# Inputs with the contracted dimension first, and expert values as 512 moving columns, in a one-core decoder-layer step

## What is computed

```python
z = h @ w_in                                  # [a | u | v], token mixing, then @ w_out, layer norm
mk, mv = mem_prompt @ w_mk, mem_prompt @ w_mv # 256 memory rows
s = einsum('bthd,bmhd->bhtm', h @ w_mq, mem_k)        # prompt: mk; samples: cache_mem_k
h = layer_norm(ALPHA * h + softmax(s) @ mem_v @ w_mo)
# expert layer: 8 heads pick 16 of 128*128 experts per token
act = gelu(einsum('thkd,td->thk', peer_u[eidx], xb))
out = einsum('thk,thkd->td', gate * act, peer_v[eidx])
h = layer_norm(ALPHA * h + out)
```

## Time and profile before

| what | value |
|---|---|
| median of 3 runs | 3913.64 us (3912.26 to 3916.97) |
| the profiled execution's own time | 3911.4 us |
| its span, first to last instruction | 3909.7 us |
| mean granted clock of PE | 0.986 of 2.4 GHz |
| PE busy / weight loads | 96% / 94% |
| DVE, ACT, POOL busy | 66%, 34%, 22% |
| chain that ended last, by engine | PE 89%, DVE 4%, DMA 3%, ACT 2% |

### The profile page before, as it was taken

The page is one execution under the profiler, slowest core; times in us unless marked ns, Lnnn a source line. Parts: engine busy times, 40 slices in busy tenths (PEclk is TensorE's granted clock), DMA queues, the critical chain, the costliest instruction groups (busy, mean ns, idle before and its releaser), DMA issues.

```text
span 3909.7 us, 61245 instructions
## 1 busy us (share of the span) xinstructions
PE 3772.0 (96%) x23909; PEld 3664.8 (94%) x23909; DVE 2585.0 (66%) x3393; ACT 1324.3 (34%) x1615; POOL 860.6 (22%) x534
## 2 busy tenths in 40 slices
PE   8998999989889989999999999999899999999997
PEld 6788999989859989999999999999899999999997
DVE  3323334352463366689888477778799989889896
ACT  3343222241442242233555322222233333333334
POOL 0000023300002300066000121223333333433440
PEclk9999999999999999999999999999999999999999
DMA  6541333323543322344455999999999999999994
GB/s 225 204 147 51 89 83 83 92 66 118 215 151 86 86 67 76 100 148 148 146 189 192 356 397 398 398 397 378 385 407 414 400 402 398 370 412 411 400 397 149
DMA packets 392373, 941.45 MB, mean 241 GB/s; under 512 B 24484, under 2 KB 264800, under 8 KB 340120
## 3 DMA queue, kind: packets, MB, share of 16 engines
q1 hardware_dynamic: 340640, 565.78, 41.6%
q0 software_dynamic: 51616, 374.19, 23.6%
HBM read 865.84 MB, written 72.77 MB: 240 GB/s over the span
## 4 chain that ended last, share of the span: by engine, by line
PE 89%; DVE 4%; DMA 3%; ACT 2%; issue 1%; DVEq 1%; POOL 0%; SPq 0%; ACTq 0%
PE pp L200 24%; PE pp L1218 24%; PE pp L1265 13%; PE pt L1265 7%; PE pl L1265 7%; PE pt L1192 2%; PE pp L844 2%; DMA u_raw<-in_peer_ut 1%; PE pt L844 1%; PE pl L844 1%; DVE vs_lo L1868 1%; DVE gbuf L2073 1%; PE pl L1140 1%; PE pp L1069 1%; PE pt L927 1%
## 5 line engine op out<-in xcount | busy, mean ns | idle before, releaser
L1218 PE MATMUL pp<-h_hi,ut_hi 128*128 128x384 f32 x2048 | 704.3, 344 | 4.2 <-DVE ut_lo L1969 4.2
L1218 PE MATMUL pp<-h_lo,ut_hi 128*128 128x384 f32 x2048 | 690.8, 337 | 0.0
L1218 PE MATMUL pp<-h_hi,ut_lo 128*128 128x384 f32 x2048 | 688.9, 336 | 0.0
L229 DVE TENSOR_TENSOR w_lo<-raw,w_hi 128x2048 fp32r<-128x2048 f32 x116 | 266.5, 2298 | 447.3 <-ACT w_hi L210 447.3
L1969 DVE TENSOR_TENSOR ut_lo<-u_raw,ut_hi 128x1024 fp32r<-128x1024 f32 x256 | 331.6, 1298 | 250.2 <-ACT ut_hi L1583 171.3
L1615 ACT ACTIVATE v_hi<-v_raw 128x1024 fp32r<-128x1024 f32 x256 | 271.8, 1062 | 657.6 <-PE pp L1265 477.7
L1218 PEld LDWEIGHTS pp<-h_hi,ut_hi 128*128 128x128 f32 x2048 | 386.0, 188 | 5.6 <-DVE ut_lo L1969 5.2
L1218 PEld LDWEIGHTS pp<-h_lo,ut_hi 128*128 128x128 f32 x2048 | 385.9, 188 | 0.0
L1218 PEld LDWEIGHTS pp<-h_hi,ut_lo 128*128 128x128 f32 x2048 | 385.2, 188 | 0.0
L2096 DVE TENSOR_TENSOR v_lo<-v_raw,v_hi 128x1024 fp32r<-128x1024 f32 x256 | 313.5, 1225 | 103.6 <-ACT v_hi L1615 102.6
L210 ACT ACTIVATE w_hi<-raw 128x2048 fp32r<-128x2048 f32 x116 | 222.0, 1913 | 388.9 <-PE pp L200 260.8
(11 more groups left out here) (431 smaller groups left out, 7879.5 us busy)
## 6 DMA issues: line engine op xcount, KB each, us to landing
u_raw<-in_peer_ut SPq DMA_DIRECT2D x256, 512.0 KB
v_raw<-in_peer_v SPq DMA_DIRECT2D x256, 512.0 KB
p_f<-p_scr SPq DMA_DIRECT2D x64, 768.0 KB
raw<-in_w_in SPq DMA_DIRECT2D x24, 1024.0 KB, 5.7
g_scr<-gs POOLq DMA_DIRECT2D x6, 4096.0 KB, 13.8
raw<-in_w_mk SPq DMA_DIRECT2D x16, 1024.0 KB, 4.8
raw<-in_w_mv SPq DMA_DIRECT2D x16, 1024.0 KB, 4.8
raw<-in_w_out SPq DMA_DIRECT2D x16, 1024.0 KB, 5.9
```

The source lines that it names most:

```text
L229: nc.vector.tensor_tensor(w_lo[:, s], raw[:, s], w_hi[:, s].bitcast(F32), ALU.subtract).then_inc(lo_ready, 1)
L1218: last = mm(pp[0][:, d, 0:N], w[:, d, k, :], x[:, k, S:S + N], start=(k == 0 and w is ut_hi and x is h_hi), stop=(k == KC - 1 and w is ut_lo))
```

## The change

Host side: x, mem_prompt and cache_mem_k are handed over with the contracted dimension in the partitions. All turns of rows, and of cached keys, are gone; ACT and DVE split from the loaded tile. x is split between the splits of panels 18 to 21. The order of k's turn and the start of the w_in panels stays otherwise.

```diff
-            for n in range(2):
-                rows_load(n)
+            sp.dma_start(quarter(mem_raw, 0), quarter(a["mem_t"], 0)).then_inc(mem_in[0], 16)
             panel_load(streams[0][1], 0)(num(1), 1)
+            for n in range(1, 4):
+                sp.dma_start(quarter(mem_raw, n), quarter(a["mem_t"], n)).then_inc(mem_in[n], 16)
...
-                    for m in range(2, len(row_tiles) - 1):
-                        rows_load(m)
+                    for m in range(4):
+                        sp.dma_start(quarter(x_raw, m), quarter(a["x_t"], m)).then_inc(x_in, 16)
...
+                    for m in range(2 * DB):
+                        if m >= 4:
+                            sp.wait_ge(kr_d, 2 * (m - 3))
+                        sp.dma_start(ckt[:, m % 4]..., a["cache_kt"][m // 2, m % 2]).then_inc(ckt_in[m % 4], 16)
+                        if m == 5:
...
+                if st == 0 and k % NG == 0:
+                    pe.wait_ge(rows_l, k // NG + 1)
...
+            def x_out(n):
+                act.wait_ge(x_in, 64)
+                f(quarter(h_hi, n), quarter(x_raw, n), ACT.Copy).then_inc(rows_h, 1)
...
-                f(kr_hi[n % 3][:, :, :], (pt2, pl)[n % 2]..., ACT.Copy)
+                f(kr_hi[n % 3][:, :, :], ckt[:, n // 2 % 4, n % 2], ACT.Copy).then_inc(kr_a, 1)
```

```diff
+            def value_tile(s, b, d, t):
+                for p, v in ((p_hi, v_hi), (p_hi, v_lo), (p_lo, v_hi)):
+                    for h in range(2):
...
+                        last = mm(acc_bank(s, t, h), p[:, d, t * P:(t + 1) * P], v[:, d, h * 512:(h + 1) * 512],
+                                  start=(b == 0 and p is p_hi and v is v_hi), stop=(b == NK - 1 and p is p_lo))
...
+            def own_rows(s):
+                pe.wait_ge(r_ready, KC + 1)
+                for t in range(ND):
+                    for c in range(8):
+                        mm(acc_bank(s, t, c // 4)[:, c % 4 * P:(c % 4 + 1) * P],
+                           r[:, 8 * s + c, S + t * P:S + (t + 1) * P], ident[:, :], start=False, stop=False)
...
-            pe.wait_ge(acc_done, KC)
             for t in range(ND):
...
+                for d in range(4):
+                    pe.wait_ge(lo_done, 2 * (2 * NK - 4 + d + 1))
+                    value_tile(1, NK - 4 + d, d, t)
...
+            for t in range(ND):
+                for h in range(2):
+                    act.wait_ge(vd_done, 2 * (ND + t) + h + 1)
+                    last = f(row_part(1, t, h), acc_bank(1, t, h)..., ACT.Copy,
+                             accum_out=rst[:, 2 + t, 1 + h:2 + h])
+                last.then_inc(ln_act, 1)
+                row_square(2 + t, row_tile(t))
                 row_std(2 + t, P)
...
-            for c in range(8, KC):
-                add_out(c)
```

More of the change, by code:

```diff
@@ L365, in program, with quarter @@
         mem_lo = at("mem_lo", Y_HI + KC * MEM * 4, [P, KC, MEM], FR)
[L366 to L370, removed]
-        NG = KC // 4
[L373 to L377, removed]
+        mem_raw = at("mem_raw", H_LO, [P, KC, MEM])
+        x_raw = at("x_raw", Y_LO, [P, KC, T])
+        NG = KC // 4
+        def quarter(x, n):
+            return x[:, NG * n:NG * (n + 1), :]
         kv_nat = [at("k_nat", TMP, [P, MT, D]), at("v_nat", Y_HI, [P, MT, D])]
@@ L818, in _ @@
             mm, turn = nc.tensor.matmul, nc.tensor.transpose
[L819 to L833, removed]
             def memory_rows(st, k):
@@ L1072, in _ @@
             pe.wait_ge(evacuated, MO0)
[L1073 to L1077, removed]
+            for n in range(DB * AH):
+                cache_scores(n)
             pe.wait_ge(two_ready, 2)
@@ L1252, in values @@
             def values(s, i, d):
-                m = i * 4 + (s * NK + d)
                 b = i * 4 + d if isinstance(i, int) else None
                 pe.wait_ge(lo_done, i * 8 + 2 * (s * NK + d + 1))
[L1257 to L1268, removed]
+                for t in range(ND):
+                    last = value_tile(s, b, d, t)
@@ L1277, in _ @@
+            for d in range(4):
+                values(0, 0, d)
+            with pe.Fori(1, NK // 4 - 1) as i:
+                for d in range(4):
+                    values(0, i, d)
+            own_rows(0)
+            for d in range(4):
+                values(0, NK // 4 - 1, d)
+            for d in range(4):
+                values(1, 0, d)
+            own_rows(1)
+            with pe.Fori(1, NK // 4 - 1) as i:
                 for d in range(4):
-                    values(s, NK // 4 - 1, d)
@@ L1281, in _ @@
-            pe.wait_ge(acc_done, KC)
+                    values(1, i, d)
             for t in range(ND):
[L1283 to L1288, removed]
+                for d in range(4):
+                    pe.wait_ge(lo_done, 2 * (2 * NK - 4 + d + 1))
+                    value_tile(1, NK - 4 + d, d, t)
@@ L1327, in _ @@
                             .then_inc(evacuated, 1)
-            for n in range(MT, len(row_tiles)):
-                rows_out(n)
             for g in range(8):
@@ L1611, in v_split @@
                     if e == 3:
-                        act.wait_ge(vd_done, 8)
+                        for t in range(ND):
+                            for h in range(2):
+                                act.wait_ge(vd_done, 2 * t + h + 1)
+                                f(row_part(0, t, h), acc_bank(0, t, h).rearrange("p (c n) -> p c n", n=P), ACT.Copy,
+                                  accum_out=rst[:, 2 + t, h:h + 1]).then_inc(acc_done, 1)
                 else:
@@ L2129, in _, with mean_of @@
             base = done[0]
-            def mean_of(t, n, parts):
+            def mean_of(t, n):
                 dve.wait_ge(ln_act, ACT_LN[f"sum{t}"])
                 x = rst[0:n, t]
-                for k in range(1, parts):
-                    tt(x[:, 0:1], x[:, 0:1], x[:, k:k + 1], ALU.add)
+                if t >= 2:
+                    stt(x[:, 0:1], x[:, 0:1], x[:, 1:2], x[:, 2:3], ALU.add, ALU.add)
                     dve.drain()
@@ L2147, in row_gain, with row_bias @@
                 stt(x, x, rst[0:n, t, 3:4], gain, ALU.add, ALU.mult)
-            def row_bias(t, n, x, bias):
+            def row_bias(t, n, x, bias, out=None):
                 dve.drain()
-                stt(x, x, rst[0:n, t, 6:7], bias, ALU.mult, ALU.add).then_inc(row_ready, 1)
-            def row_out(t, n, x, gain, bias):
-                row_gain(t, n, x, gain)
-                row_bias(t, n, x, bias)
+                stt(x if out is None else out, x, rst[0:n, t, 6:7], bias, ALU.mult, ALU.add).then_inc(row_ready, 1)
             def by_chunk(x):
@@ L2189, in _ @@
             for m in range(2, 2 * NK):
-                if m == NK + 3:
-                    for c in range(8):
-                        add_out(c)
+                if m == NK + 5:
+                    dve.wait_ge(acc_done, 2 * ND)
+                    tt(rst[:, 2:5, 0:1], rst[:, 2:5, 0:1], rst[:, 2:5, 1:2], ALU.add)
+                    dve.drain()
                 v_split(m)
```

231 lines of the change are left out of this document (105 added, 126 removed).

## The result

| | before | after |
|---|---|---|
| median of the runs, us | 3912.95 (4 runs, 3909.51 to 3916.97) | 3870.16 (4 runs, 3867.26 to 3872.23) |
| ratio after / before | | 0.9893, 95% interval 0.9881 to 0.9905 |
| profiled execution, us (its span) | 3911.40 (3909.7) | 3867.26 (3865.5) |

The change gains 42.8 us where 66 were forecast; 3870.2 lies just above the range of 3834 to 3870.

A forecast was written before the change was run, and what follows sets the result against it. PE, working 96% of the span, was taken as the bound. Terms 5.5 + 12.9 + 17.4 + 21.6 - 5.4 + 14.2 = 66.2 us took 3911.4 to 3845.2 us profiled, 3847 as a median; range 3834 to 3870.

The forecast's parts named there:

- the part on the values: Value products: 18 matmuls of 512 columns replace 24 of 384 per block; minus 21.6 us, bounds 8 and 28.
- Columns alone set the pace: Rival on the values: 512 columns take 231.5 ns, the block stays at 4.167 us; 3869 us, chance 0.05.
- Own rows: Values: 48 added float32 matmuls of 128 columns at 0.113 us; plus 5.4 us, bounds 3.1 and 10.9.
- start: Kernel start: PE begins 10.2 us sooner, but panel 6 is ready near 55; minus 5.5 us, bounds 0 and 10.2.
- turns of x: Between v's evacuation and the first w_in panel: x split during panels 18 to 21; minus 12.9 us, bounds 10 and 14.
- tail: Behind PE's last product: 13.7 us instead of 29.1, less 1.1 for stalls; minus 14.2 us, bounds 8 and 17.
- cached keys: Cached-key scores: turns gone, DVE and then DMA limit, scores end at 1047.5; minus 17.4 us, bounds 23.3 and 4.
- the stop for a load behind `ktp`: Cached keys: with `ktp` in small pieces before load 6, 3 us of stall are added.
- The rival of the clock: Cached keys run largely at half clock, PE 1.86 us a pair, scores end at 1061; 3860 us, chance 0.10.
- DMA did not cap the values: Rival on the values: DMA caps them and two thirds of the gain would go; 3861 us, chance 0.13.
- Nor did DVE bind there: Rival on the values: DVE becomes the bound, a block at 4.40 us, slower than before; 3925 us, chance 0.02.

The follow-up runs named there:

- e3: The changed kernel with p_lo alone moved by 192 bytes; 3843.60 us in one run, 3850.95 us (ratio 0.9848) when timed again in five runs.
- e5: A separate program, TensorE alone on zero operands at different start offsets, against no kernel; 512 columns took 226.7 ns aligned, up to 233.4 ns otherwise.
- e7: The changed kernel without its products of own rows with the scaled identity; 3862.89 us in one run.
- e8: The changed kernel with the ktp loads issued behind all sixteen loads of cached keys instead of behind the sixth; 3858.45 us in one run.
- e11: The changed kernel with p_lo moved 192 bytes, ktp loads behind all cached keys, and tiles h and y 64 bytes lower; 3837.49 us, ratio 0.9807.
- e2: The changed kernel with the loop over the two 512-column halves moved outside the three value products; 3865.89 us in one run.
- e4: The changed kernel with both the halves loop outside the three value products and p_lo moved by 192 bytes; 3849.83 us in one run.

## Why the prediction was wrong

The step that failed stands in the part on the values: "The extra is 12.0, 13.6 and 13.4 ns, a constant. So a block costs 18 x 226.7 = 4.080 us". The three extras came from three stages with their operands in different places. 13.4 ns was that of the memory rows, whose four tiles start alike; carried to the values it was right for a kernel in which `p_lo` starts alike too (e3: exactly 226.7), and wrong for this one. The values gained 3.4 us instead of 21.6. The rival "Columns alone set the pace" hit the number, 231.5 ns and 3869 us, at a chance of 0.05, and its mechanism was wrong: aligned, 512 columns do take 226.7 (e3, e5). The bounds of the term, 8 and 28 us, were worked out for extras of 16 or 12 ns (16 would leave 9.9, not 8); 17.8 was outside, though the trace of before had a warning: the u products with the same 384 columns stood 175.6 ns apart, the values 173.9. Two paces for one shape say that something besides the shape decides. The prediction took one of them and never set it beside the other.

The Trainium skill ("TensorE: Matmul & The Clock Gate", section "Back-to-back issue gap") gives N/2.4 + 2.5 ns, 215.8 for 512 columns. No order and no place here came under 226.7, so that the trace does not agree. The Trainium skill's page "SBUF — State Buffer", section "Operand start alignment", lets an operand start at any multiple of its element size and says of its runs that they timed nothing; e5 shows that the legal places differ by up to 6.7 ns a matmul.

**Own rows** were mis-sized: 48 products at the price of 48 turns, 5.4 us. A float32 product against the identity takes two records where the turn takes one; 10.7 us by the trace and 9.0 to 10.7 by e7, up to nearly the upper bound of 10.9.

Right, by their own steps: the **start** (5.6 for 5.5, with the spread told above; panel 6 at 55.8 where "near 55" was worked out, the load issued at 40.5 for "near 40"); the **turns of x** (12.8 for 12.9); the **tail** (12.5 us behind the end of the last product, where 13.7 were forecast, and one stop of 1.9 us for 1.8; its own sum, 29.1 - 13.7 - 1.1, is 14.3 and not 14.2). The **cached keys** gave 15.5 of 17.4: the shape was right, transfers and DVE in turns, but the stop for a load behind `ktp` was 4.6 us and not 3 (e8). The rival of the clock came true in small: with the lower level granted, a pair takes PE 1.7 us, near the 1.86 of that rival, and PE bounds the stage; but that holds for some 10 of its 48 us (0.90 granted over all of it), and behind the stop it cost 1.2 us. DMA did not cap the values: with `p_lo` moved they ran faster at 412 GB/s. Nor did DVE bind there: 182 of 200 us busy in e3, and PE full.

In sum, 18.2 us (pace) and 5.3 us (own rows) were missing, and about 1.5 came back in the other terms.

## What to carry to other kernels

Work out the distance between matmul starts for each stage by itself, and where one shape shows two paces, compare the start addresses of its stationary and moving tiles within 256 bytes before giving a price to a new shape. Lay split operands (hi and lo) at the same place within 256 bytes; it costs a shift of one allocation, and for 512 columns here it decided whether a rewrite of the value products was worth 20 us or 3. Price a float32 product against the identity at twice a turn (1.78 us for 8, against 1.81 for 16 turns in the earlier trace rows).

## What the runs showed of the hardware

- Two operands of fp32r, the type of the split tiles, that start alike within 256 bytes: 32 cycles at 2.4 GHz beside the columns for 384 and 512 columns; up to 48 cycles otherwise (233.4 ns for 512; e5). For 272 columns the aligned pair is not the best: 125.4 ns, and 123.3 with the stationary tile 64 bytes further. What in the chip does this was not found out. Neither was a layout tried that puts the 272-column products at 123.3 ns; 2 ns on each of the 8448 would be some 17 us, an estimate from the 125.3 ns of the earlier trace rows and the 123.3 of e5.
- The pace of a mixture is not the mean of its parts. Two aligned products to one with the stationary tile 64 bytes off stand 231.1 ns apart, not 228.9 (e5). In e11 the u products alternate, chunk by chunk, between offsets that e5 has at 173.3 and 174.6 ns, and the mean was 173.3, not 174.0. What rule gives these numbers was not found out.
- An order of products (banks in turn, the same stationary tile twice in a row) makes no difference that the trace can show: 231.1 ns in both orders (e2), 226.7 in both (e3, e4).
